# Two transformer blocks on one core: large tiles moved to multiples of 512 bytes

## The reference, cut to what matters

```python
def swiglu(x, w1, w2):
    gu = x @ w1
    g, u = gu[..., :D_FF_2], gu[..., D_FF_2:]
    return (jax.nn.silu(g) * u) @ w2

def second_block(...):
    for l in range(DEPTH):
        x = x + 0.5 * swiglu(rms_norm(x, ffn1_norm[l]), ffn1_w1[l], ffn1_w2[l])
        x = x + hybrid_mixer(rms_norm(x, mix_norm[l]), ...)
        x = x + 0.5 * swiglu(rms_norm(x, ffn2_norm[l]), ffn2_w1[l], ffn2_w2[l])
    return rms_norm(x, final_norm)
```

## The kernel before

| tiles | before: past 512 | past 64 | after: past 512 | past 64 |
|---|---|---|---|---|
| xT, raw, w_hi, w_lo, w_sums | 128 | 0 | 0 | 0 |
| ident, ones, rot_pe, causal | 128 | 0 | 128 | 0 |
| params | 160 | 32 | 128 | 0 |
| rs, rs_b, cosT, sinT, X | 160 | 32 | 0 | 0 |
| REGION_A: a_hi, a_lo, more_hi, more_lo, late_hi | 160 | 32 | 0 | 0 |
| REGION_B: h_hi, h_lo, seven_x, early_hi, early_lo, mixers' tiles | 160 | 32 | 0 | 0 |

## Time and profile before

### The profile page before, as it was taken

How to read it: one execution, slowest core, us unless ns; L and a number is a source line. 1 busy time by engine, 2 the same in 40 slices (tenths; PEclk the granted TensorE clock), 3 DMA queues, 4 the chain that set the end, 5 groups by cost and what they waited for, 6 DMA issues and landing times.

```text
span 3521.9 us, 49474 instructions
## 1 busy us (share of the span) xinstructions
PE 3430.8 (97%) x19557; PEld 2899.5 (82%) x19557; DVE 2464.7 (70%) x3512; ACT 1618.0 (46%) x2387; POOL 56.0 (2%) x84
## 2 busy tenths in 40 slices
PE   7999999999999999999999999999999989999999
PEld 5679987668998799887677799889988757778987
DVE  8668854759872888457895688458863888658853
ACT  4545533445652456226523355425542552335642
POOL 1000000000000000000000000000000000000000
PEclk9999999999999999999999999999999999999999
DMA  4123323212332233332132233323333213322332
GB/s 139 54 67 96 108 85 108 88 44 82 108 108 96 72 108 109 99 99 57 48 96 84 96 96 108 99 93 96 109 102 95 74 44 95 85 96 84 108 102 84
DMA packets 339642, 318.95 MB, mean 91 GB/s; under 512 B 31768, under 2 KB 312164, under 8 KB 339428
## 3 DMA queue, kind: packets, MB, share of 16 engines
q1 hardware_dynamic: 335588, 307.95, 28.1%
q0 software_dynamic: 2048, 6.16, 0.5%
q10 hardware_dynamic: 1792, 1.88, 0.2%
HBM read 313.84 MB, written 2.10 MB: 90 GB/s over the span
## 4 chain that ended last, share of the span: by engine, by line
PE 84%; DVE 12%; ACT 2%; issue 1%; ACTq 0%; POOL 0%; DMA 0%; DVEq 0%; POOLq 0%
PE products L791 34%; PE products L932 25%; PE products L830 7%; PE small L830 6%; PE small L932 4%; PE products L1193 2%; DVE seven_x L2398 1%; PE products L1390 1%; DVE w_lo L2146 1%; DVE x_sums L2387 1%; DVE X L2166 1%; PE small L1267 1%; PE products L1283 1%; DVE mla_prob L2593 1%; ACT w_hi L1516 1%
## 5 line engine op out<-in xcount | busy, mean ns | idle before, releaser
L2146 DVE TENSOR_TENSOR w_lo<-raw,w_hi 128x2048 fp32r<-128x2048 f32 x190 | 435.1, 2290 | 505.8 <-ACT w_hi L1516 505.4
L1516 ACT ACTIVATE w_hi<-raw 128x2048 fp32r<-128x2048 f32 x190 | 363.6, 1914 | 871.0 <-PE products L791 607.7
L791 PE MATMUL products<-a_hi,w_hi 128*128 128x512 f32 (+1 forms) x1216 | 495.7, 408 | 10.3 <-DVE a_lo L2206 9.5
L791 PE MATMUL products<-a_lo,w_hi 128*128 128x512 f32 (+1 forms) x1216 | 482.4, 397 | 0.0
L791 PE MATMUL products<-a_hi,w_lo 128*128 128x512 f32 (+1 forms) x1216 | 482.1, 396 | 0.0
L932 PE MATMUL products<-seven_x,w_hi 128*128 128x256 f32 x2592 | 468.3, 281 | 5.0 <-ACT h_full L1625 3.0
L932 PEld LDWEIGHTS products<-seven_x,w_hi 128*128 128x128 f32 x2592 | 398.6, 189 | 8.4 <-ACT h_full L1625 4.2
L932 PE MATMUL products<-seven_x,more_hi 128*128 128x256 f32 x1632 | 381.4, 283 | 1.8 <-ACT rs_b L1625 1.8
L932 PE MATMUL products<-seven_x,w_lo 128*128 128x256 f32 x1296 | 364.6, 281 | 0.0
L791 PEld LDWEIGHTS products<-a_hi,w_hi 128*128 128x128 f32 (+1 forms) x1216 | 228.9, 188 | 73.7 <-issue 14.7
L932 PEld LDWEIGHTS products<-seven_x,more_hi 128*128 128x128 f32 x1632 | 282.2, 191 | 2.4 <-ACT rs_b L1625 2.4
(11 more groups left out here) (463 smaller groups left out, 7263.4 us busy)
## 6 DMA issues: line engine op xcount, KB each, us to landing
raw<-in_ffn_w SPq DMA_DIRECT2D x244, 512.0 KB, 4.3
raw<-in_w_in SPq DMA_DIRECT2D x108, 512.0 KB, 4.8
raw<-in_w_ffn_in SPq DMA_DIRECT2D x88, 512.0 KB, 4.4
raw<-in_w_ffn_out SPq DMA_DIRECT2D x40, 512.0 KB, 4.5
raw<-in_w_out SPq DMA_DIRECT2D x32, 512.0 KB, 4.1
raw<-in_ffn_w SPq DMA_DIRECT2D x24, 384.0 KB, 3.6
raw<-in_w_mem_kv SPq DMA_DIRECT2D x8, 512.0 KB, 4.0
raw<-in_lru_w_out SPq DMA_DIRECT2D x8, 512.0 KB, 3.5
```

Of the source, the lines that this page charges most:

```text
L791: mm = pe.matmul(G[pair][0:m, into + b, 0:n], w[:, s, at:at + m], x, start=(first or into > 0) and k == 0 and q == 0, stop=(last or ends) ...
L1516: act.activation(w_hi[:, s, :], raw[:, s, :], ACT.Copy).then_inc(hi_ready, 1)
L2146: dve.tensor_tensor(w_lo[:, s, :], raw[:, s, :], w_hi[:, s, :].bitcast(F32), ALU.subtract).then_inc(lo_ready, 1)
```

## The change

All large tiles are placed after the small ones. `params`, whose size is a multiple of 512, now stands ahead of `freq`. After the last small tile the next free address is rounded up to a multiple of 512 (LINE). From there on follow `rs`, `rs_b`, `cosT`, `sinT`, `X`, `xT`, `raw`, `w_hi` and `w_lo`, and then the two regions as before, all with sizes that are multiples of 512. REGION_A moves from 105632 to 105984 and REGION_B from 138400 to 138752. Nothing else is changed: each engine has the same instructions in the same order with the same waits, and each DMA the same shape.

```diff
+LINE = 512
@@
     KB = 1024
+    ident = place("ident", [P, P])
+    ones = place("ones", [P, P])
+    rot_pe = place("rot_pe", [P, P])
+    causal = place("causal", [P, SEQ])
+    params = place("params", [P, n_param_tiles * P])
+    freq = place("freq", [P, 2])
+    stats = place("stats", [P, 4, 32])
...
+    minus_half = place("minus_half", [P, len(GROUPS) * TC])
+    top[0] = -(-top[0] // LINE) * LINE
+    rs = place("rs", [P, SEQ])
+    BROADCASTS = top[0]
+    rs_b = place("rs_b", [P, SEQ])
+    final_gain = place("final_gain", [P, D], at=top[0])
+    cosT = place("cosT", [P, SEQ])
+    sinT = place("sinT", [P, SEQ])
+    X = place("X", [P, 4, SEQ])
     xT = place("xT", [P, DC, SEQ])
     raw = place("raw", [P, 2, UNIT])
     W_HI = top[0]
@@
     w_sums = place("w_sums", [P, 2, UNIT], at=W_LO)
-    ident = place("ident", [P, P])
...
-    freq = place("freq", [P, 2])
-    params = place("params", [P, n_param_tiles * P])
...
-    rs = place("rs", [P, SEQ])
-    BROADCASTS = top[0]
-    rs_b = place("rs_b", [P, SEQ])
-    final_gain = place("final_gain", [P, D], at=top[0])
-    cosT = place("cosT", [P, SEQ])
-    sinT = place("sinT", [P, SEQ])
-    X = place("X", [P, 4, SEQ])
     ROWS_4 = 10 * P
```

More of the change, by code:

```diff
@@ L265, in two_blocks @@
     KB = 1024
+    ident = place("ident", [P, P])
[5 more added lines that the diff above has]
+    stats = place("stats", [P, 4, 32])
+    sinks = place("sinks", [P, DEPTH * WINDOW_HEADS])
+    minus_sinks = place("minus_sinks", [P, DEPTH * WINDOW_HEADS])
+    decay = place("decay", [P, 2, DEPTH * LC])
+    tiny = place("tiny", [P, 6, DEPTH * LC])
+    mean_sq = place("mean_sq", [P, len(GROUPS) * TC])
+    minus_half = place("minus_half", [P, len(GROUPS) * TC])
[7 more added lines that the diff above has]
+    X = place("X", [P, 4, SEQ])
     xT = place("xT", [P, DC, SEQ])
@@ L272, in two_blocks @@
     w_sums = place("w_sums", [P, 2, UNIT], at=W_LO)
-    ident = place("ident", [P, P])
-    ones = place("ones", [P, P])
-    rot_pe = place("rot_pe", [P, P])
-    causal = place("causal", [P, SEQ])
-    freq = place("freq", [P, 2])
-    params = place("params", [P, n_param_tiles * P])
[L279 to L285, removed]
-    rs = place("rs", [P, SEQ])
-    BROADCASTS = top[0]
-    rs_b = place("rs_b", [P, SEQ])
-    final_gain = place("final_gain", [P, D], at=top[0])
-    cosT = place("cosT", [P, SEQ])
-    sinT = place("sinT", [P, SEQ])
-    X = place("X", [P, 4, SEQ])
     ROWS_4 = 10 * P
```

## The result

The changed kernel takes **3500.48 us** (median of 5 runs, 3497.09 to 3502.43) against 3523.54 us for the kernel before, measured beside it (5 runs, 3520.19 to 3525.65). The ratio is 0.9932, with an interval of 0.9921 to 0.9943: 0.68% faster. The prediction, 3514.6 us with a range from 3505 to 3528, had the direction and 40% of the size, and its range does not hold the measured time.

What follows compares the result with a forecast made beforehand. TensorE's matmul count times pace was taken as the bound. One term, 9.1 us saved with all others at 0, took the span from 3521.9 to 3512.8 us; 1.8 us for the median gave 3514.6, range 3505 to 3528.

Steps and rivals of the forecast that it cites:

- What bounds the kernel: Whole kernel: TensorE, busy 3430.8 of 3521.9 us, sets the time by matmul count times pace, besides stage entries.
- I read this as a load that costs a little more when its 512 bytes per partition don't begin on a multiple of 64: Seven-product stage: weights off a multiple of 64 cost P3, P4 and P5 28 ns a product, 2.3 ns a matmul.
- the rival on equal offsets: Matmuls: operands starting equal within 64 bytes collide, slowing the kernel to 3535.8 us, up to 3559; chance 0.09.
- The term of 9.1 us saved: Seven-product stage: 324 products with misplaced weights (P3, P4, P5) each get 28 ns faster, 9.1 us in all.
- (b): The other 432 products and all 512-column matmuls: weights already aligned or load hidden, so change taken as 0.
- The excess over the clock: All matmuls: 8.6% above the 2.4 GHz pace; offset within 512 bytes could remove up to 295 us, chance 0.01.
- (c): VectorE and ScalarE: no gain from the new offsets; they wait for TensorE, so a few ns would not show.
- (d): DMAs: faster landing is worth nothing within stages, only the start waits; taken as 0, bounds 0 to 0.6 us.
- (f): TensorE's clock: half-clock share comes from idle gaps at stage entries, which stay; taken as 0, 2 us allowed either way.
- The rule on lines of 16 bytes: SBUF operands: no extra line is crossed before, so the change is worth 0; supports no change, 3523.7 us, chance 0.23.
- The 215.7 ns for 512 columns: 512-column matmuls: the skill's pace on another data type, cited beside the 233.3 ns here; no run shown reached it.

Runs made afterwards that it cites:

- experiment 1: Kernel of matmuls alone, all computation left out, stretches of 48 differing only in operand starts; equal starts at (0, 0): 226.7 ns at 512 columns, 120.0 at 256.
- experiment 3: Two variants of the changed kernel: large tiles 32 bytes further, 3502.46 us (ratio 0.9938); rounding to 512 dropped, 3497.65 us (0.9937).
- experiment 7: Kernel of matmuls alone, stretches of 60 at 256 columns (some at 512), each behind four different preceding stretches; at distance 192: 113.3, 117.8, 117.8, 113.3 ns.
- experiment 6: Changed kernel with large tiles on multiples of 256 and the seven-product stage's moving tiles 32, 64 or 192 bytes later: 3477.51, 3482.58, 3455.44 us.

## Why the prediction was wrong

- **What bounds the kernel: right.** TensorE's pace times its count, with the entries of stages beside it. All of the 24 us is pace, minus what the entries took back. That the time moved the way that was forecast is luck all the same: the term that was to bring it had the other sign, and the gain came from a term that I had put at 0.
- **"I read this as a load that costs a little more when its 512 bytes per partition don't begin on a multiple of 64": the step that failed.** The reading of the earlier trace rows was sound in its numbers: 1.433 against 1.405 us. But in that stage two things vary together, as the rival on equal offsets said: the three products have weights 32 off and distance 0, the four others weights on a multiple of 64 and distance 32. I gave the first the credit. Experiments 1 and 3 have weights at 0 and at 32 with the same distance and the same pace: that misplacement costs nothing. What cost time in its place was distance 0 at 256 columns, 120.0 ns a matmul. The longer loads of `more_hi` go with the slower pace and not with the place. After, those of `w_hi` are as long:

```profile
L934 PEld LDWEIGHTS products<-seven_x,w_hi 128*128 128x128 f32 x2592 | 404.5, 192 | 11.0 <-DVE w_lo L2429 4.4 <-ACT h_full L1627 3.9 <-DVE w_lo L2437 2.4
...
L934 PEld LDWEIGHTS products<-seven_x,more_hi 128*128 128x128 f32 x1632 | 283.8, 192 | 3.6 <-ACT rs_b L1627 3.6
```

  Mean ns of one is the number before the second bar: 192 for both. The term of 9.1 us saved was in fact 2.3 us lost (324 x 7 ns).
- **(b), "The other 432 products and all 512-column matmuls … I take 0": both halves wrong.** The 432 products lost 15.1 us, the 512-column matmuls gained 56.5. Of the earlier trace rows I wrote that "neither the one misplacement nor the other shows, or both show equally". There was a third reading: the two stages have distances 32 and 224 and neither has 0, so both could pay for the distance. The rows of before have no 512-column stage at distance 0, so they could not tell what it would give; they could tell that it was untested, and the term of 0 with its bounds should have had a gain among them that didn't need a misplaced operand.
- **The excess over the clock.** I wrote that the excess over 2.4 GHz, 8.6% at 512 columns, "grows with the columns, which a start cannot do". The relative start takes a good part of it: 226.7 ns in place of 233.3 is a third of the excess of 20 ns, and at 256 columns 113.3 in place of 117.1 is 3.8 of 10.4. Its effect doesn't simply grow with the columns either (nothing between distances 0 and 32 at 384). The rest of the excess no run here touched. That a start could not do this rested on no row.
- **(c), VectorE and ScalarE: right.** Busy 2465.5 and 1615.9 us, where they were 2464.7 and 1618.0. The two subtractions of the earlier trace rows take 1226 and 1219 ns, 1 ns more each; that they still differ by 7 ns says that the offset was not what set them apart.
- **(d), DMAs: right within the stages, short at the start.** raw's median landing went from 4.3 to 4.2 us, and all that is waited for it is 0.4 us, once. The waits at the start fell from 8.3 to 7.8 and from 2.6 to 1.8, 1.3 us in all, where I had bounded the gain by 0.6. The rule of the Trainium skill in "DMA: Bandwidth & Descriptors", section "How a descriptor splits into AXI transactions", has the sign of this, though it tells of bytes that are fetched and these tiles are written; one profiled execution each doesn't show more.
- **(f), the clock: right.** The mean granted clock was 0.992 before and is 0.993.
- **The rival on equal offsets** had the seven-product stage right, down to its own deciding point (the loads of `w_hi` from 189 to 191, measured 192) and nearly its price: 12.1 us forecast for the 432 w products, 15.1 measured, rounds of 10.03 forecast and 10.08 measured. It was wrong at 512 columns, where it carried the same sign over: a loss of up to 23 us forecast, a gain of 56.5 measured. I gave it 0.09 against the loads of X at 192 ns with `ones` 32 away; those are matmuls of one column, and experiment 1 shows that the effect changes with the number of columns and is absent at 128. What bears on 256 columns must be read at 256 columns.
- **The rule on lines of 16 bytes** (the Trainium skill, "SBUF — State Buffer", section "Specifications (TRN2)") would have made the change worth 0. The trace disagrees: 233.3 to 226.7 ns with every operand on a multiple of 32 before and after. A start off a multiple of 16 was the slowest at 256 columns (123.3 ns, experiment 1), so lines of 16 may count as well; they aren't all.
- **The 215.7 ns for 512 columns** of the Trainium skill, "TensorE: Matmul & The Clock Gate", section "Wait — 56ns, not 53.3ns?", measured on another data type, was not reached: the best pace of any run here is 226.7.

## What to carry to other kernels

On a kernel that TensorE bounds, the distance between where the weights and the moving columns begin, modulo 256 bytes, is a free parameter, worth 0.7 to 2.3% here: measure the pace of a stretch of back-to-back matmuls over all distances in the shape that the kernel uses, choose by stage, and prefer a distance whose pace is the same in every stretch. When the stages of one profile, or the executions of one kernel, disagree by more than the others do, look at each stage by itself before believing a mean. If two quantities vary together in all rows of a trace (here the place of the weights and its distance to the moving columns), a difference belongs to neither until a run or a row separates them; a group of rows in which neither value of the tested quantity occurs says nothing about it. A small tile between two large ones can decide this, so an experiment that undoes the named part of a change (here the rounding to 512) is worth its run.

## What was not expected of the hardware

- **The pace of float32r matmuls (the data type of all split tiles) depends on the relative start of their two operands, with a period of 256 bytes:** 226.7 to 236.7 ns at 512 columns (the 236.7 was seen at distance 240, in experiment 7), 113.3 to 120.0 at 256 columns, and 123.3 at a distance of 4. The best distance for one is among the slowest for the other: 0 gives 226.7 and 120.0. At 128 and 384 columns (0, 0) and (0, 32) don't differ. This was seen with starts on multiples of 32; (16, 16) took 230.0 and 118.3, so there the place counts too, or distance 0 has a second pace.
- **Some distances have two steady paces or more, with the same operands and instructions:** at 256 columns 113.3 or 117.8 ns at distances 64 and 192, 116.7 or 117.8 at 32; at 512 columns 228.9 or 233.3 at 64, and 226.7, 233.3 or 236.7 at 240. The pace holds through a whole stage: 18 rounds of 84 matmuls in experiment 6.
- **VectorE and ScalarE show none of it.** The two subtractions took 1225 and 1218 ns before, 1226 and 1219 after; ScalarE was busy for 1618.0 us before and 1615.9 after.

That two reads share something in SBUF that repeats every 256 bytes, and meet or miss each other by their phase, would fit the period. No run shows it: it is argued only. What makes the pace fall into the one or the other state, and why 512 columns want distance 0 and 256 columns 112, stays open. The rest of the excess at 512 columns (226.7 against 213.3 ns) doesn't come from the choice of output bank: distance 0 took 226.7 in banks 5, 6, 7 and 0 in experiment 7. Whether it depends on the step between the weights' slices was not tried.
